# Zero-padded 128-column expert operands, and the third expert's tokens found by one-hot products, in a fused encoder block

## The reference

```python
logits = hf @ w_router + b_router
top_val, top_idx = lax.top_k(logits, 4)
gates = jax.nn.softmax(top_val, axis=-1)
# tokens are grouped by expert; for each group xb of expert e:
gu = xb @ w_gu[e] + b_gu[e]                       # 1024 -> 2048
x_glu = jnp.minimum(gu[:, :1024], 7.0)
x_lin = jnp.clip(gu[:, 1024:], -7.0, 7.0)
act = x_glu * jax.nn.sigmoid(1.702 * x_glu) * (x_lin + 1)
y = act @ w_down[e] + b_down[e]                   # 1024 -> 1024
# out[token] += gate * y, then x = x + out and a final RMS norm
```

## Time and profile before

| | |
|---|---|
| three timed runs | 1919.34 us median (1916.19 to 1920.76) |
| profiled execution | 1919.02 us, its span 1917.2 us |
| mean granted TensorE clock | 0.971 of full speed |
| busy in the span | TensorE 93%, its loads 68%, VectorE 74%, ScalarE 57%, GpSimd 26% |
| chain that ended last | TensorE 87%, VectorE 6%, DMA 2%, GpSimd 2% |
| largest lines in that chain | L1658 35%, L1678 19%, L1378 to L1380 25% |

### The profile page before, as it was taken

How to read it: one execution, slowest core, us unless ns; L and a number is a source line. 1 busy time by engine, 2 the same in 40 slices (tenths; PEclk the granted TensorE clock), 3 DMA queues, 4 the chain that set the end, 5 groups by cost and what they waited for, 6 DMA issues and landing times.

```text
span 1917.2 us, 23304 instructions
## 1 busy us (share of the span) xinstructions
PE 1783.2 (93%) x8227; PEld 1312.3 (68%) x8227; DVE 1415.1 (74%) x1292; ACT 1085.4 (57%) x996; POOL 500.2 (26%) x334
## 2 busy tenths in 40 slices
PE   5999769999988959899999999999999999999992
PEld 4887458889875736677777777777777777777761
DVE  4423982335433658799999999999999999999994
ACT  4132663234224226677777777777777777777762
POOL 3000000000000007134334335335335335335321
PEclk9999999999989969999999999999999999999996
DMA  9222113324530336899999999999999999999983
GB/s 308 80 88 88 28 61 139 108 88 153 175 93 1 122 137 254 311 359 367 375 376 365 379 372 369 377 372 367 379 370 371 379 367 373 378 365 375 377 308 105
DMA packets 111061, 501.35 MB, mean 262 GB/s; under 512 B 9365, under 2 KB 9434, under 8 KB 78154
## 3 DMA queue, kind: packets, MB, share of 16 engines
q1 hardware_dynamic: 98752, 459.30, 62.6%
q0 software_dynamic: 10784, 36.46, 7.6%
q10 hardware_dynamic: 1482, 5.01, 0.7%
HBM read 478.40 MB, written 22.34 MB: 261 GB/s over the span
## 4 chain that ended last, share of the span: by engine, by line
PE 87%; DVE 6%; DMA 2%; POOL 2%; issue 2%; ACT 1%; ACTq 0%; DVEq 0%; SPq 0%; POOLq 0%
PE ps L1658 35%; PE ps L1678 19%; PE ps L1378 9%; PE ps L1379 8%; PE ps L1380 8%; POOL slot_table L612 2%; PE ps L1647 1%; DVE zexp L1057 1%; PE ps L1627 1%; PE ps L1636 1%; PE ps L1583 1%; PE ps L1667 1%; PE ps L1557 1%; DVE wts L1072 1%; DMA raw<-in_w_in 1%
## 5 line engine op out<-in xcount | busy, mean ns | idle before, releaser
L1205 DVE TENSOR_TENSOR wlo<-raw,whi 128x2048 fp32r<-128x2048 f32 x380 | 854.5, 2286 | 85.8 <-ACT whi L867 81.9
L867 ACT ACTIVATE whi<-raw 128x2048 fp32r<-128x2048 f32 x380 | 718.3, 1914 | 173.9 <-PE ps L1658 164.5
L587 POOL TENSOR_TENSOR mark<-ident 1x1 f32<-1x1 f32 x32 | 228.3, 7136 | 332.5 <-ACT ybuf L889 332.5
L1658 PE MATMUL ps<-whi,xhi 128*96 128x512 f32 x1024 | 287.4, 402 | 2.7 <-DVE xlo L1210 2.7
L957 DVE TENSOR_TENSOR wlo<-raw,whi 128x2048 fp32r<-128x2048 f32 x52 | 117.3, 2289 | 224.7 <-ACT whi L659 224.7
L1658 PE MATMUL ps<-wlo,xhi 128*96 128x512 f32 x1024 | 279.5, 394 | 0.0
L1658 PE MATMUL ps<-whi,xlo 128*96 128x512 f32 x1024 | 279.0, 394 | 0.0
L1658 PEld LDWEIGHTS ps<-wlo,xhi 128*96 128x96 f32 x1024 | 166.2, 162 | 71.8
L1658 PEld LDWEIGHTS ps<-whi,xlo 128*96 128x96 f32 x1024 | 166.2, 162 | 71.8
L1658 PEld LDWEIGHTS ps<-whi,xhi 128*96 128x96 f32 x1024 | 163.7, 163 | 71.5 <-issue 2.9
L1678 PE MATMUL ps<-whi,ahi 128*96 128x512 f32 x512 | 167.4, 408 | 0.0
(11 more groups left out here) (296 smaller groups left out, 2282.0 us busy)
## 6 DMA issues: line engine op xcount, KB each, us to landing
raw<-in_w_gu SPq DMA_DIRECT2D x256, 1024.0 KB, 8.2
raw<-in_w_down SPq DMA_DIRECT2D x128, 1024.0 KB, 7.4
raw<-in_w_in SPq DMA_DIRECT2D x14, 1024.0 KB, 6.9
raw<-in_w_gate SPq DMA_DIRECT2D x8, 1024.0 KB, 5.3
raw<-in_w_xkv SPq DMA_DIRECT2D x8, 1024.0 KB, 5.1
raw<-in_w_attn_up SPq DMA_DIRECT2D x4, 1024.0 KB, 5.6
raw<-in_w_out SPq DMA_DIRECT2D x4, 1024.0 KB, 5.5
raw<-in_w_xq SPq DMA_DIRECT2D x4, 1024.0 KB, 7.1
```

The source lines that it names most:

```text
L587: g.tensor_tensor(mark[:, 0:1], ident[0:1, 0:1], ident[0:1, 1:2], ALU.add)
L867: s.activation(whi[:, m % RING, :], raws[m % RAWS], ACT.Copy).then_inc(hi_done, 1)
L1205: v_.tensor_tensor(wlo[:, m % RING, :], raws[m % RAWS], whi[:, m % RING, :].bitcast(F32), ALU.subtract).then_inc(lo_done, 1)
L1658: mm = t_.matmul(ps[0:CAP, n, :], a[:, k, :], w[:, slot, n * 512:(n + 1) * 512], start=False, stop=k == KT - 1 and a is xlo)
```

## The change

Three edits.

1. The expert operands `xhi`, `xlo`, `ahi`, `alo` and the selectors `sel_gu`, `sel_dn` get 128 columns in place of 96. Columns 96 to 127 are zeroed once by POOL. The matmuls of `gate_up` and `down` use all 128 columns as the stationary operand and write all 128 partitions of PSUM; rows 96 to 127 are never read. The transposes and the elementwise work keep 96.
2. The third expert's indices also come from one-hot products (`FIRST = 3`). VectorE makes 12 one-hot tiles rather than 8, TensorE makes the third set of products after the counts, into the bank of the second. POOL gathers the third expert's tokens ahead of the 16 table DMAs.
3. `turn_x(2)` moves from behind `gate_up(1)` into its middle, and the split of the second expert's tokens moves: on ScalarE ahead of the sigmoid, on VectorE between the two evictions and the two products of the first gate.

```diff
+FIRST = 3
-        xhi = at("xhi", 100, [P, KT, CAP], F32R)
+        xhi = at("xhi", 100, [P, KT, P], F32R)
...
-        sel_gu = at("sel_gu", 182, [3 * E, CAP], BF16)
+        sel_gu = at("sel_gu", 182, [3 * E, P], BF16)
...
-        first_sel = at("first_sel", 140, [P, 2, TT, CAP])
+        first_sel = at("first_sel", 116, [P, FIRST, TT, CAP])
...
+            g.memset(sel_gu[:, CAP:], 0.0).then_inc(pads_zeroed, 1)
+            g.memset(sel_dn[:, CAP:], 0.0).then_inc(pads_zeroed, 1)
             select(sel_gu, 0, sel_gu_ready)
             select(sel_dn, 0, sel_dn_ready)
             pool.wait_ge(hf_stored, 16 * TT)
+
+            pool.wait_ge(rlT_ps, 1)
+            for operand in (xhi, xlo, ahi, alo):
+                g.memset(operand[:, :, CAP:].bitcast(F32), 0.0).then_inc(pads_zeroed, 1)
             gather_first(0)
 
             pool.wait_ge(x_turned, 1)
             gather_first(1)
 
             select(sel_gu, 1, sel_gu_ready, gu_biased, 1)
+
+            pool.wait_ge(first_ready, 3)
+            g.tensor_copy(idx_cur[:, :], first_idx[:, 2:3]).then_inc(idx_copied, 1)
+            pool.wait_ge(x_turned, 2)
+            pool.wait_ge(idx_copied, 1)
+            g.indirect_dma_start(out=xg[:, :], out_offset=None, in_=hf_rows,
+                                 in_offset=bass.IndirectOffsetOnAxis(ap=idx_cur[:, :], axis=0)).then_inc(gathered, 16)
...
-            gather(2, 1, 2)
             select(sel_dn, 1, sel_dn_ready, dn_biased, 1)
             select(sel_gu, 2, sel_gu_ready, gu_biased, 2)
             gather(3, 2, 3)
@@ ScalarE
             for j in range(4, 12):
                 if j == 11:
+                    act.wait_ge(unit_used, U + 8)
+                    x_part(2)
                     gate(1)
-                    x_part(2)
@@ VectorE
-            def gate(i1, used_value):
+            def gate(i1, used_value, between=None):
...
+                if between is not None:
+                    between()
                 dve.wait_ge(glu_ready, i1)
...
-            for e in range(2):
+            for e in range(FIRST):
                 for t in range(TT):
                     v_.tensor_scalar(first_sel[:, e, t, :], iota_s[:, :], rank[:, t, e:e + 1], chosen[:, t, e:e + 1],
...
             link(v_.tensor_copy(counts[:, :], ps[:, 5, 0:E]))
+            first_index(2, 4)
...
-                    gate(1, U + 8)
-                    x_part(2)
+                    gate(1, U + 8, between=lambda: x_part(2))
@@ TensorE
+            first_slots(0, 3)
+            first_slots(1, 4)
             for t in range(TT):
                 mm = t_.matmul(ps[:, 5, 0:E], ones[:, :], chosenb[:, t, :], start=t == 0, stop=t == TT - 1)
             mm.then_inc(count_ps, 1)
+            pe.wait_ge(first_ready, 2)
+            first_slots(2, 4)
...
-                            mm = t_.matmul(ps[0:CAP, n, :], a[:, k, :], w[:, slot, n * 512:(n + 1) * 512], start=False,
+                            mm = t_.matmul(ps[:, n, :], a[:, k, :], w[:, slot, n * 512:(n + 1) * 512], start=False,
...
             turn_x(1)
-            gate_up(1, U + 1)
-            turn_x(2)
+            pe.wait_ge(pads_zeroed, 6)
+            gate_up(1, U + 1, halfway=lambda: turn_x(2))
```

More of the change, by code:

```diff
@@ L215, in build @@
         xg = at("xg", 96, [CAP, D])
-        xhi = at("xhi", 100, [P, KT, CAP], F32R)
-        xlo = at("xlo", 104, [P, KT, CAP], F32R)
+        xhi = at("xhi", 100, [P, KT, P], F32R)
+        xlo = at("xlo", 104, [P, KT, P], F32R)
         glu = at("glu", 108, [CAP, D])
@@ L221, in build @@
         hid = at("hid", 120, [CAP, D])
[L222 to L223 removed]
+        ahi = at("ahi", 124, [P, KT, P], F32R)
+        alo = at("alo", 136, [P, KT, P], F32R)
         ybuf = at("ybuf", 140, [CAP, D])
@@ L1209, in x_part @@
                 dve.wait_ge(x_hi, i1)
[L1210 to L1211 removed]
+                v_.tensor_tensor(xlo[:, :, 0:CAP], ps[:, 6:8, :].rearrange("p b (k n) -> p (b k) n", n=P)[:, :, 0:CAP],
+                                 xhi[:, :, 0:CAP].bitcast(F32), ALU.subtract).then_inc(x_ready, 1)
             def a_part(i1):
                 dve.wait_ge(a_hi, i1)
[L1215 to L1218 removed]
+                v_.tensor_tensor(alo[:, :, 0:CAP], ps[:, 6:8, :].rearrange("p b (k n) -> p (b k) n", n=P)[:, :, 0:CAP],
+                                 ahi[:, :, 0:CAP].bitcast(F32), ALU.subtract).then_inc(a_ready, 1)
+            def gate(i1, used_value, between=None):
                 dve.wait_ge(unit_used, used_value)
@@ L1264, in _, with first_index @@
                                      ALU.is_equal, ALU.mult).then_inc(first_sel_ready, 1)
-            for e in range(2):
+            def first_index(e, bank):
                 dve.wait_ge(first_ps, e + 1)
-                v_.tensor_copy(first_idx[:, e:e + 1], ps[0:CAP, 3 + e, 0:1]).then_inc(first_ready, 1)
+                v_.tensor_copy(first_idx[:, e:e + 1], ps[0:CAP, bank, 0:1]).then_inc(first_ready, 1)
+            first_index(0, 3)
+            first_index(1, 4)
             dve.wait_ge(count_ps, 1)
@@ L1608, in _, with first_slots @@
             mm.then_inc(rank_ps, 1)
-            for e in range(2):
+            def first_slots(e, bank):
                 for t in range(TT):
                     pe.wait_ge(first_sel_ready, TT * e + t + 1)
-                    mm = t_.matmul(ps[0:CAP, 3 + e, 0:1], first_sel[:, e, t, :], tokf[:, t:t + 1], start=t == 0,
+                    mm = t_.matmul(ps[0:CAP, bank, 0:1], first_sel[:, e, t, :], tokf[:, t:t + 1], start=t == 0,
                                    stop=t == TT - 1)
                 mm.then_inc(first_ps, 1)
+            first_slots(0, 3)
+            first_slots(1, 4)
             for t in range(TT):
@@ L1646, in gate_up @@
                 for n in range(4):
-                    mm = t_.matmul(ps[0:CAP, n, :], sel_gu[:, :], bias3[:, n * 512:(n + 1) * 512], start=True, stop=False)
+                    mm = t_.matmul(ps[:, n, :], sel_gu[:, :], bias3[:, n * 512:(n + 1) * 512], start=True, stop=False)
                 mm.then_inc(gu_biased, 1)
@@ L1666, in down @@
                 for n in range(2):
-                    mm = t_.matmul(ps[0:CAP, 4 + n, :], sel_dn[:, :], bias3[:, 2 * D + n * 512:2 * D + (n + 1) * 512],
+                    mm = t_.matmul(ps[:, 4 + n, :], sel_dn[:, :], bias3[:, 2 * D + n * 512:2 * D + (n + 1) * 512],
                                    start=True, stop=False)
@@ L1677, in down @@
                                 c = kk * D + n * 512
-                                mm = t_.matmul(ps[0:CAP, 4 + n, :], a[:, k, :], w[:, j, c:c + 512], start=False,
+                                mm = t_.matmul(ps[:, 4 + n, :], a[:, k, :], w[:, j, c:c + 512], start=False,
                                                stop=k == KT - 1 and a is alo)
```

15 lines of the change are left out of this document (8 added, 7 removed).

## The result

The changed kernel took 1896.03 us (median of four runs, 1893.76 to 1896.46) against 1920.05 us; the ratio is 0.9869 with a 95% interval of 0.984 to 0.9898. The forecast was 1897.1 us. The profiled execution took 1896.39 us, its span is 1894.3 us, 22.9 us less than before. The forecast's sum was 21.9 us (19.4 + 2.5). About that came, but not from its terms.

The account below looks back on a forecast made before the run. TensorE alone, through the spacing of its matmuls, was taken to bound the experts' loop at full clock. 1919.0 - 19.4 (columns) - 2.5 (start) = 1897.1 us; range 1886 to 1908.

Parts of the forecast that it names:

- The columns, 19.4 us: Expert matmuls: 128 stationary columns bring the spacing from 230.9 to 226.7 ns, saving 4.2 ns on each of 4608.
- a period becomes 35.28 us: Loop over the experts: one expert's period falls from 35.88 us by 0.60 to 35.28 us.
- The bounds: Limits on the width's gain: 120 us cost if the load's 26 ns came through; nothing if 373 GB/s is the ceiling.
- the slower rival: Expert matmuls: the wider load's 26 ns add to each spacing, giving 2037 us; chance 0.04.
- Width nothing: Loop: weights or VectorE set the pace at 35.9 us, or the 4.2 ns belong elsewhere; 1913 to 1917 us, chance 0.12.
- The start, 2.5 us beyond the width's: Start of the experts: gate-up 3 begins 5.6 us earlier; after clock restart and the width's 1.0, 2.5 us are left.
- The steps up to gate-up 3: Start of the experts: first index 1.0 us later, gate-up 2 at 743.3, third expert's 6.52 us wait gone, gate-up 3 wanted 777.7 (780.7).
- a selector copy that misses the gate: POOL's queue: selector copy held until 784.6 by VectorE's subtractions; gate-up 3 begins at 785 after 7 us of TensorE idleness.
- my range of 773.6 to 778.6: POOL's queue at the start of the experts: when the table read is issued, after 16 table DMAs and 5.06 us landing.
- The gate of 769.9: VectorE's second gate: starts at 769.9, 4.2 us after gate-up 2, and lasts 5.7 us, to 775.6.
- the first rival: Start of the experts: POOL's wait short or absent, winning 6 to 12 us beyond the width's; 1893.6 to 1888, chance 0.37.
- The gate's products: VectorE's gate: its two-input products did not block POOL's table DMAs (0.97 us each, against 6.09 beside unbroken subtractions).

Follow-up runs that it names:

- e8: Kernel before with 128-column tiles (token slices 512 bytes apart for 384) but matmuls over 96 columns: 1917.82 us, ratio 0.9978 to the kernel before.
- e2: Changed kernel with the expert and bias matmuls using 96 of the 128 columns: 1912.01 us, ratio 0.9947 to the kernel before.
- e3: Changed kernel with the expert and bias matmuls using 112 of the 128 columns: 1909.02 us, ratio 0.9921 to the kernel before.
- e9: Changed kernel with the expert and bias matmuls using 124 of the 128 columns, run once: 1901.84 us, ratio 0.990 to the kernel before.
- e10: Changed kernel with 64 columns used, leaving out tokens in slots 64 to 95, run once: 1922.17 us, ratio 1.001 to the kernel before.
- e7: e4 with POOL's copy of `ycur` ahead of the fourth gather: 1893.67 us, ratio 0.9853 to the kernel before.
- e4: Changed kernel with three of the 16 table DMAs ahead of the third expert's gather on POOL's queue: 1891.28 us, ratio 0.9845 to the kernel before.
- e6: Changed kernel with the split of the second expert's tokens behind the first gate again: 1896.25 us, ratio 0.9867 to the kernel before.
- e1: Kernel before with only the width changed (128-column tiles, zeroing and matmuls): 1909.93 us, ratio 0.9927 to the kernel before.

## Why the prediction was right, point by point

**The columns, 19.4 us.** Right in kind; the spacing is that of the dense row to 0.1 ns in the down products. The size was off: the loop from gate-up 4 has 4224 of the 4608 products, 17.7 us by the forecast, and gave 14.8. The step that was mis-sized is "a period becomes 35.28 us"; it is 35.39. The spacing of 226.7 ns was taken for all 144, but the first products of a gate-up group come further apart (up to 236 ns): the gate-up products take 10.91 and 10.96 us for 48, not 10.88, and the bias 0.88 for 0.86. The series shows that columns do it, from 96 to 124, and e8 that 0.12 us of the 0.48 are the distance between slices, which the prediction had not seen as a separate thing: it varied two things and named one. Why more columns go with a closer spacing stays open; no run here tells it. The rule of the Trainium skill (TensorE: Matmul & The Clock Gate, Weight-path perf modes) that a quick load needs all 128 weights and a type that is not FP32 does not explain it. Were it to apply to this format, the gain would come between 124 and 128 columns, but 124 columns already have the 226.7 ns of 128 in the down products, and the load only grows with the width.

**The bounds.** The 26 ns of the longer load did not come through at all; the slower rival falls with every run of the series from 96 columns up. Width nothing falls too: at 381 GB/s no landing is late, so 373 GB/s was no ceiling.

**The start, 2.5 us beyond the width's.** It gave 8.6 us, of which about 1.6 to the width (384 matmuls at 4.2 ns): 7 us. The steps up to gate-up 3 held: the four more one-hot tiles made the first index 0.96 us later, gate-up 2 began at 743.4 (forecast 743.3), down 1's transposes at 767.6 (765.7, or 768.7 with a fallen clock), the bias of gate-up 3 at 779.6 (777.7 or 780.7). These times hold the 0.8 us that the dense part took more; less that, gate-up 2 came 0.7 us ahead of the forecast, since POOL had issued the first gather 0.87 us after its index before (705.54 to 706.41), and now 0.28 us after it (707.28 to 707.56). The clock did fall, for a shorter stretch: four products took 2.07 us, and the granted clock from 743 to 747 was 0.57.

```profile
743.00:747.00 4.00, 4.00 (x12) 2.99 (x11) 3.96 (x4) 2.03 (x2) 3.39 (x3) 0.57 0.27 104
```

The step that failed is "a selector copy that misses the gate". The read-back was issued at 773.00, ahead of my range of 773.6 to 778.6: behind gate 1 stood a run of three subtractions (745.58 to 752.27), not five, and the table DMA beside it took 5.35 us, less than the 6.09 of before. And the gate came later (771.97 to 777.68 for 769.9 to 775.6), so the selectors made it. What is behind them did not: the index copy was held instead, and the price reached TensorE by way of `ycur`, ScalarE and VectorE. It was 3.5 us (38.9 from gate-up 3 to gate-up 4 instead of 35.4), not the 7 and a fallen clock of the forecast. The gate of 769.9 had been worked out for a clock that stays high; for the fallen clock, which the prediction also gave, it is 772.9 to 778.6, and then its whole range for the read-back lies inside the gate. What came is the first rival (short wait, 1888 to 1893.6), and by the start alone it was the better forecast. The loop gave 2.9 us less than its part and the start 4.5 more (7.0 for 2.5); that two misses of opposite sign left the time within about 1 us of 1897.1 is luck.

The mechanism of the forecast is real: it is what e2, e3 and e9 do, with TensorE idle 7.03 us in e2 and a start of 120 us in all three. Which of the two happens goes with when the read-back is issued against a gate of 5.7 us; no run moves the read-back alone. Ordered by how long the read-back was issued ahead of the run of four: e2 (0.4 us behind it), e9 (2.0 us ahead) and e3 (2.2) have a selector held and a start of 120 us; e10 (2.9), the changed kernel (4.7) and e7 (5.2) have the index copy held; e4 (8.1) and e6 (8.3) only `ycur`. So about 6 us of this kernel's time hang on an alignment that no edit aims at.

**The gate's products.** The prediction says that they did not block POOL. For the table DMAs that is so: 0.97 us beside them. POOL's small copies did wait for them: in e6 the index copy took 0.95 us for 0.18 and ended with a product, and in e3 `sel_dn` took 0.98 us for 0.28, so that `sel_gu` behind it came too late.

**Parts of the change do not add.** Width alone has a start 4.5 us longer in its profiled execution, the third expert's products give 10.3 us with the others in place, the split gives nothing.

## What to carry to other kernels

When one engine is the bound without a gap, read the spacing of its instructions in every stage and compare forms that differ in one thing: here 4 ns in 231 was 15 us, and it went against the length of the loads.

When a wait is removed, follow the queue that held it to its end. A small copy on GpSimd costs 0.3 us or 8 us by whether it meets a gap in VectorE's work, so put the long chain first into the time in which its engine idles: moving three DMAs ahead of a wait took away a stall worth 3.5 us.

When a time is split into a spacing, take the spacing from inside the group: 11.19 us over 48 products reads as 233.1 ns, and the products were 230.0 ns apart.

## What the runs showed of the hardware

- Stationary columns and matmul spacing (128 rows, 512 moving columns, 4-byte format, full clock): 64, 96, 112, 124, 128 columns gave 230.0, 230.0, 229.0, 226.7 and 226.7 ns in the down products behind the first few of a group, with loads of 135, 162, 176, 185 and 188 ns. 64 columns cost 0.12 to 0.15 us more at each change to or from the bf16 bias products. Slices 384 bytes apart rather than 512 cost 1 ns more at 96 columns (11.08 to 11.09 for 11.04 us in 48).
- While VectorE ran four subtractions of two SBUF tiles back to back, POOL's copies did not finish: 7.64, 8.06, 8.30, 8.88 and 9.7 us (e3, e9) for copies that take 0.2 to 0.3 us else. The Trainium skill (SBUF — State Buffer, SBUF: two separate sides) says that one holds the shared ports for a whole instruction. For these copies the trace goes further: POOL did not get in between one subtraction and the next in a run of four, only behind the run. A table DMA did: issued at 745.54 beside a run of three (745.58 to 752.27), it ended at 750.89, 1.4 us before the third did. In e2 one beside such a run (744.99 to 751.68) took 7.56 us, to 752.51.
- The clock fell to 1.2 GHz between experts 1 and 2 in every run: in the eight with one idle stretch of 2.54 us there (the changed kernel among them) it was low for 3.4 us, in the four with two stretches (before, e1, e6 and e8; 2.53 and 2.40 us in e6) for 6.8 us. In the changed kernel the granted clock is 0.50 from 743.34 to 746.74 and 1.00 on either side.
